# The rope part of the first attention's scores in two passes of the array instead of three

## What is computed

```python
q = (rmsnorm(c_q_raw, q_norm) @ w_uq).reshape(B, S, H, NOPE_DIM + ROPE_DIM)
kv = (rmsnorm(c_kv_raw, kv_norm) @ w_ukv).reshape(B, S, H, NOPE_DIM + V_DIM)
k_nope, v = kv[..., :NOPE_DIM], kv[..., NOPE_DIM:]
q_rope = apply_rope(q[..., NOPE_DIM:], cos[:, :, None, :], sin[:, :, None, :])
k_rope = apply_rope(k_rope_raw, cos, sin)
q_full = jnp.concatenate([q[..., :NOPE_DIM], q_rope], axis=-1)
k_full = jnp.concatenate(
    [k_nope, jnp.broadcast_to(k_rope[:, :, None, :], (B, S, H, ROPE_DIM))], axis=-1)
...
s = jnp.einsum('bqhd,bkhd->bhqk', q_blk, k).astype(jnp.float32) * scale
s = jnp.where(k_idx[None, :] <= q_idx[:, None], s, jnp.finfo(jnp.float32).min)
pr = jax.nn.softmax(s, axis=-1)
```

## Time and profile before

| | |
|---|---|
| median of 3 runs | 1946.9 us (1946.67 to 1947.23) |
| profiled execution, its own time | 1946.78 us |
| its span in the trace | 1945.0 us |
| PE busy | 1925.1 us (99%) |
| DVE busy | 1226.0 us (63%) |
| ACT busy | 898.4 us (46%) |
| POOL busy | 536.3 us (28%) |
| mean clock granted to TensorE | 0.999 of full |

### The profile page before, as it was taken

One profiled execution on the slowest core, in us unless ns is written; L12 is line 12 of the kernel. 1 busy time (PEld: TensorE's weight loads), 2 busy tenths in 40 slices (PEclk: granted clock), 3 DMA queues, 4 the chain that ended last, 5 costly groups with the idle time before them and its releaser, 6 DMA issues.

```text
span 1945.0 us, 23730 instructions
## 1 busy us (share of the span) xinstructions
PE 1925.1 (99%) x9278; PEld 1605.7 (83%) x9278; DVE 1226.0 (63%) x1697; ACT 898.4 (46%) x1309; POOL 536.3 (28%) x396
## 2 busy tenths in 40 slices
PE   8999999999999999999999999999999999999998
PEld 7777878888888888888888888888888888888886
DVE  6657676538236845545455857667666676766757
ACT  7445543424235442525255544434455555444435
POOL 2333552251415435353533000000333341000000
PEclk9999999999999999999999999999999999999999
DMA  5312356575532323231315657364322226746553
GB/s 165 95 44 76 101 122 161 136 150 141 101 108 87 109 66 109 66 108 65 108 65 152 155 154 188 109 184 120 108 86 86 86 66 184 181 122 173 127 176 87
DMA packets 164690, 229.70 MB, mean 118 GB/s; under 512 B 4784, under 2 KB 108976, under 8 KB 164464
## 3 DMA queue, kind: packets, MB, share of 16 engines
q1 hardware_dynamic: 148192, 195.24, 32.7%
q0 software_dynamic: 16096, 32.01, 9.5%
q10 hardware_dynamic: 304, 1.12, 0.2%
HBM read 223.23 MB, written 4.72 MB: 117 GB/s over the span
## 4 chain that ended last, share of the span: by engine, by line
PE 94%; DVE 3%; ACT 2%; issue 0%; DMA 0%; SPq 0%; POOL 0%; ACTq 0%; DVEq 0%
PE ps L1150 30%; PE ps L1151 29%; PE ps L1152 29%; PE ps L1322 1%; PE ps L1352 1%; PE ps L1361 1%; PE ps L1362 1%; ACT scr L2255 1%; PE ps L1339 1%; PE ps L1855 0%; DVE x L3243 0%; DMA raw<-in_w_in 0%; DVE hid_lo L3089 0%; DVE hn_lo L3247 0%; ACT w_hi L2008 0%
## 5 line engine op out<-in xcount | busy, mean ns | idle before, releaser
L1150 PE MATMUL ps<-hn_hi,w_hi 128*128 128x512 f32 (+1 forms) x1556 | 607.6, 391 | 4.0 <-DVE hn_lo L3192 1.7
L1152 PE MATMUL ps<-hn_hi,w_lo 128*128 128x512 f32 (+1 forms) x1556 | 599.5, 385 | 0.0
L1151 PE MATMUL ps<-hn_lo,w_hi 128*128 128x512 f32 (+1 forms) x1556 | 599.4, 385 | 0.0
L1004 POOL TENSOR_TENSOR w_lo<-raw,w_hi 128x512 fp32r<-128x512 f32 x244 | 343.0, 1438 | 517.8 <-ACT w_hi L2000 517.8
L1150 PEld LDWEIGHTS ps<-hn_hi,w_hi 128*128 128x128 f32 x1556 | 292.7, 188 | 66.4 <-issue 4.8
L1152 PEld LDWEIGHTS ps<-hn_hi,w_lo 128*128 128x128 f32 x1556 | 292.5, 188 | 59.3
L1151 PEld LDWEIGHTS ps<-hn_lo,w_hi 128*128 128x128 f32 x1556 | 292.8, 188 | 57.2 <-issue 1.4
L1150 PE MATMUL ps<-w_hi,hid_hi 128*128 128x512 f32 x616 | 240.0, 390 | 0.2
L1151 PE MATMUL ps<-w_lo,hid_hi 128*128 128x512 f32 x616 | 239.7, 389 | 0.0
L1152 PE MATMUL ps<-w_hi,hid_lo 128*128 128x512 f32 x616 | 239.7, 389 | 0.0
L2044 ACT ACTIVATE w_hi<-raw 128x1024 fp32r<-128x1024 f32 x112 | 116.1, 1055 | 205.7 <-PE ps L1152 205.4
(11 more groups left out here) (383 smaller groups left out, 2902.7 us busy)
## 6 DMA issues: line engine op xcount, KB each, us to landing
raw<-in_mlp_w SPq DMA_DIRECT2D x56, 1024.0 KB, 5.5
raw<-in_ret_w_in SPq DMA_DIRECT2D x24, 1024.0 KB, 5.1
aux<-in_mlp_w POOLq DMA_DIRECT2D x16, 1024.0 KB, 9.2
raw<-in_att_w_in SPq DMA_DIRECT2D x12, 1024.0 KB, 5.3
raw<-in_w_gate SPq DMA_DIRECT2D x11, 1024.0 KB, 5.4
raw<-in_w_up SPq DMA_DIRECT2D x11, 1024.0 KB, 5.3
raw<-in_w_down SPq DMA_DIRECT2D x9, 1024.0 KB, 5.2
raw<-in_ret_w_out SPq DMA_DIRECT2D x8, 1024.0 KB, 5.1
```

The source lines that it names most:

```text
L1004: ins = pool.tensor_tensor(w_lo[:, slot, at], raw[:, slot, at], w_hi[:, slot, at].bitcast(F32), ALU.subtract)
L1150: pe.matmul(o, hi, rhs_hi, start=start, stop=False, skip_group_check=True)
L1151: pe.matmul(o, hi, rhs_lo, start=False, stop=False, skip_group_check=True)
L1152: return pe.matmul(o, lo, rhs_hi, start=False, stop=stop, skip_group_check=True)
```

## The change

The rope rows of each query head are laid out anew: 32 rows of the high part and under them the 32 rows of the low part, in the 64 partitions of that head's half (`Q_ROPE`, `q_rope_rows`). Since the rope key's high part lies in all four quarters, one pass of 64 rows now gives high by high and low by high together, and a second pass of 32 rows gives high by low. To write this layout, ACT makes one full high copy per group of four heads into `sq_halves` (`rope_hi`) and four copies of 32 partitions (`rope_hi_rows`), and DVE makes four subtractions of 32 partitions (`rope_low`) where it had one of 128. The order of the steps on both engines changes too, and so do PE's waits ahead of tile 3 of pairs 0 and 2.

```diff
--- before.py
+++ after.py
@@ -535,6 +535,13 @@
         att_squares = [tab[:, 0, :], aux[:, 0, :], aux[:, 1, :], tmp[:, 1, :]]
         Q_NOPE_LO = (hid_hi[:, 2, :], hid_hi[:, 3, :], hid_lo[:, 2, :], hid_lo[:, 3, :])
 
+        Q_ROPE = (hid_hi[:, 9, :], hid_lo[:, 9, :], hid_hi[:, 10, :], hid_lo[:, 10, :])
+
+        def q_rope_rows(h, low):
+
+            at = 64 * (h % 2) + 32 * low
+            return Q_ROPE[h // 2][at:at + 32, :]
+
         def head_values(j):
 
             both = (hid_hi, hid_lo)[j // 2][:, 12 + 2 * (j % 2):14 + 2 * (j % 2), :]
@@ -596,9 +603,8 @@
                 r, q, k = self.rows(b), self.p, 4 + self.p
                 q_hi, q_lo = probs_t[r, q, :], Q_NOPE_LO[q][r, :]
                 nope = [(q_hi, hid_hi[r, k, :]), (q_hi, hid_lo[r, k, :]), (q_lo, hid_hi[r, k, :])]
-                r, q = slice(32 * (h % 4), 32 * (h % 4) + 32), 9 + h // 4
-                rope = [(hid_hi[r, q, :], hid_hi[r, 8, :]), (hid_hi[r, q, :], hid_lo[r, 8, :]),
-                        (hid_lo[r, q, :], hid_hi[r, 8, :])]
+                r = self.rows(b)
+                rope = [(Q_ROPE[self.p][r, :], hid_hi[r, 8, :]), (q_rope_rows(h, 0), hid_lo[64 * b:64 * b + 32, 8, :])]
                 return [nope, rope]
 
             def v_both(self, b, j):
@@ -1333,7 +1339,7 @@
                 for nth in range(2):
                     for t in tiles:
                         parts = [a.qk(b)[1 - nth] for b in range(2)]
-                        for n in range(3):
+                        for n in range(len(parts[0])):
                             for b in range(2):
                                 q, k = parts[b][n]
                                 ins = pe.matmul(a.score_ps(b, t), q[:, t * P:(t + 1) * P], k[:, 0:(t + 1) * P],
@@ -1388,7 +1394,9 @@
                     pe.wait_ge(pair_free[g.pair], g.freed(p % 2))
                     if p == 0:
                         pe.wait_ge(s["krep_done"], 96)
-                        pe.wait_ge(s["qr_lo"], 2)
+                    if p % 2 == 0:
+                        pe.wait_ge(s["qr_hi"], p + 2)
+                        pe.wait_ge(s["qr_lo"], p // 2 + 1)
                     g = UQ.group(2 + p // 2)
                     pe.wait_ge(pair_free[g.pair], g.freed(p % 2))
                     pair_scores(ONES[p], (3,))
@@ -2231,7 +2239,13 @@
             def rope_hi(r):
 
                 act.wait_ge(s["q_rope"], r + 1)
-                act.activation(hid_hi[:, 9 + r, :], tmp[:, r, :], ACT.Copy).then_inc(s["qr_hi"], 1)
+                act.activation(sq_halves[:, r, :], tmp[:, r, :], ACT.Copy).then_inc(s["qr_hi"], 1)
+
+            def rope_hi_rows(r):
+
+                for n in range(4):
+                    ins = act.activation(q_rope_rows(4 * r + n, 0), tmp[32 * n:32 * n + 32, r, :], ACT.Copy)
+                ins.then_inc(s["qr_hi"], 1)
 
             def nope_hi(n):
 
@@ -2242,9 +2256,11 @@
                         .then_inc(s["q_nope_hi"], 1)
 
             rope_hi(0)
+            rope_hi_rows(0)
             nope_hi(0)
             rope_hi(1)
             nope_hi(1)
+            rope_hi_rows(1)
             split(CONVS.chunk(1))
 
             def pair_exps(a, b):
@@ -3048,13 +3064,22 @@
                     dve.tensor_tensor(Q_NOPE_LO[tile], ps[:, g.bank(m), :], probs_t[:, tile, :].bitcast(F32),
                                       ALU.subtract).then_inc(pair_free[g.pair], 1)
 
+            def rope_low(r):
+
+                dve.wait_ge(s["q_rope"], r + 1)
+                dve.wait_ge(s["qr_hi"], 2 * r + 1)
+                for n in range(4):
+                    rows = slice(32 * n, 32 * n + 32)
+                    ins = dve.tensor_tensor(q_rope_rows(4 * r + n, 1), tmp[rows, r, :],
+                                            sq_halves[rows, r, :].bitcast(F32), ALU.subtract)
+                ins.then_inc(s["qr_lo"], 1)
+
+            rope_low(0)
             nope_low(0)
-            for r in range(2):
-                dve.wait_ge(s["q_rope"], r + 1)
-                dve.wait_ge(s["qr_hi"], r + 1)
-                dve.tensor_tensor(hid_lo[:, 9 + r, :], tmp[:, r, :], hid_hi[:, 9 + r, :].bitcast(F32),
-                                  ALU.subtract).then_inc(s["qr_lo"], 1)
             nope_low(1)
+            rope_low(1)
+            dve.wait_ge(s["qr_hi"], 4)
+            dve.wait_ge(s["qr_lo"], 2)
 
 
             def pair_masked(a, tiles, at=MASK_AT):
```

## The result

| | before | changed |
|---|---|---|
| median of 11 runs | 1946.9 us (1946.34 to 1948.14) | 1951.88 us (1950.35 to 1953.25) |
| ratio, 95% interval | | 1.0023 [1.0016, 1.0031] |
| profiled execution, its own time | 1946.78 us | 1950.35 us |
| its span | 1945.0 us | 1948.2 us |
| time less span | 1.8 us | 2.15 us |

The account below looks back on a forecast made before the run. PE, busy 99% of the span, was taken as the bound. Each pair: +0.53 us in tiles 2, 0 and 1, -0.23 in tile 3; four pairs add +1.2 to 1946.8, giving 1948.0 us, range 1944.2 to 1950.8.

Parts of the forecast that it names:

- DVE, before the first masks: Six more DVE subtractions, 3.6 us, mostly fill idle time; masks start some 0.5 us later, PE waits for nothing: price nothing.
- the third: DVE's rope subtractions run beside POOL, masks end at 89.6, PE waits 5.8 us before tiles 2, 0, 1: 1953.8 us; 4%.
- The price of one 32-partition subtraction: On DVE ahead of the first masks: each added subtraction priced at 0.60 us, six making 3.6 us.
- The masks: On DVE: first mask starts near 81.9 us with no idle time ahead, and PE shows no wait for it.
- An ACT copy of 32 partitions: On ACT: in a row every 0.5 us or so, eight new ones about 4 us, the first four from 72.1 to 74.2.
- The switch: On PE: changing a pass's row count costs 0.20 us, about 0.10 ahead to empty the array and 0.11 behind for loads.
- the rope stretch: Tiles 2, 0 and 1 of each pair, first rope to first nope pass: 1.94 us against 1.41, +0.53 us.
- tile 3: Tile 3 of each pair: switches stay three, one 512-column pass falls away, -0.23 us; 1.56 us instead of 1.79.
- Rival 1: Switches between 64 and 32 rows nearly free among rope passes: -0.63 us a pair, -2.5 us in all, 1944.3 us; 12%.
- Rival 2: Switches in close succession cost about 0.35 us instead of 0.20: 3.0 us more over four pairs, 1951.0 us; 8%.
- ACT's and POOL's delays: ACT's split of convolution chunk 1 and POOL's low part move some 2.1 us later, covered by idle time: price nothing.

Follow-up runs that it names:

- The run with DVE's part alone: Kernel before, with the rope subtractions cut into eight of 32 partitions, four ahead of nope and four behind: median 1950.3 us, ratio 1.0015.
- the run without waits: Changed kernel with DVE doing nope of heads 0-3, both rope groups, tile 3's masks, then nope of heads 4-7: median 1948.6 us, ratio 1.0008.
- nope ahead of rope: Changed kernel with DVE doing the two nope subtractions of heads 0 to 3 ahead of the four rope ones: median 1953.5 us, ratio 1.0033.
- the grouped kernel: Changed kernel with the rope passes of tiles 2, 0 and 1 ordered three of 32 rows, then three of 64: median 1948.8 us, ratio 1.0009.

## Why the prediction was wrong

**The step that failed** is "DVE, before the first masks". It priced the delay of the nope subtractions at nothing, with the sentence that the first nope group's banks come free at 78.2, "also in time". I checked that against tile 3, which wants them at 79.35, and not against what PE does ahead of it. The first convolution product starts at 76.53 and writes into these very banks. They came free at about 75.9 before the change, 0.6 us ahead of it, which no list of waits showed. The four rope subtractions in front took 2.8 us; DVE began them 0.25 us earlier than it had begun nope, so nope came 2.55 us later (77.19 against 74.64). Between the end of nope and PE's next start pass 0.15 us in the changed kernel, so the margin was 0.45 us, and 2.55 - 0.45 = 2.1 us is by how much the product starts later (78.63 against 76.53). The run with DVE's part alone shows the wait (2.02 us), and the run without waits shows 0.25 us left at this place when nope stands first.

**The rival that was nearest** was the third: DVE late, PE waits. I had it at 4%, at the wrong place (ahead of tile 2) and only through POOL. Its mechanism is real: nope ahead of rope ran into it, with the last two subtractions at 1.2 us each and a wait of 1.76 us.

**The price of one 32-partition subtraction** in a row was 0.69 us (2.77 for four), not the 0.60 that I took from the pitch of the 128x512 ones. The masks were forecast for 81.9; DVE was free for them at 82.5. In the changed kernel this cost nothing, because PE was late by then. An ACT copy of 32 partitions in a row was mis-sized too: the first four took 2.54 us (71.97 to 74.51), 0.63 each and not "0.5 us or so", and pushed the nope copies from 74.02 to 74.53. In the changed kernel DVE was busy with rope until 77.19, so nobody waited for them. Where nope stands first, it is the 0.25 us at the first convolution product.

**The clock was missing from the sum.** It has no term for it, as if the granted clock were 1.00 throughout, which it is in that stretch of the kernel before. Behind a new pause of PE of 1.8 to 2.1 us, five of eight profiles show it at 1.2 GHz for 3 to 7 us; behind 4.8 us the one profile does, and behind 0.6 us the one profile doesn't. In the changed kernel it costs 1.5 to 1.6 us where it happens, and by the mean clocks on record it happened in 8 of 24 executions. The Trainium skill says in "TensorE: Matmul & The Clock Gate", section "Why this matters for your kernels", that long idle gaps between bursts of matmuls bring the clock back down. The gaps that it names are longer than the ones of 1.8 to 2.1 us here, and behind these the clock fell all the same, to 0.58 in the stretch from 80 to 84 us of the grouped kernel; so here the measurement decides.

**What was right.** The switch as the cost that eats the gain: 1.88 us for the rope stretch (1.94 forecast), 1.55 for tile 3 (1.56). A pair costs 0.47 - 0.24 = +0.23 us by these, so +0.9 in four (+1.2 forecast). The lag behind the kernel before is 2.10 us at the first convolution matmul (78.63 against 76.53) and 3.06 us at the matmul near 189 us (191.75 against 188.69), so 0.96 us came in between, as these passes say. Rival 1 (the switch is nearly free) is refuted by grouping: the same passes in another order are 2.6 us faster. Rival 2 (a switch at 0.35 us) as well: none of them is dearer than 0.20. ACT's and POOL's delays cost nothing in the changed kernel, as said.

**The sum over the change**, then: 1.0 us of switches less passes, 2.25 us by the wait, 0.5 us of clock on average (1.5 to 1.6 us in a third of the executions), 0.1 to 0.8 us that the four profiles have behind 189 us, and 0.3 us outside the span. That makes 4.2 to 4.9 us, against 4.5 and 5.0 by the medians and 4.1 and 4.6 by the means of the same runs. The share of the clock is an estimate, from the mean clock of each execution, which is on record to three digits only. Two terms have no cause shown: the part behind 189 us, which the kernel without waits has too (0.4), and the time less span, which is 2.1 to 2.2 us in each kernel with the stacked rows and 1.8 to 1.9 in those without.

## What to carry to other kernels

When work is put in front of an instruction that frees PSUM banks, look for the next writer of those banks in PE's order, whatever it belongs to; it may be a product that has nothing to do with the change, and a small margin there shows in no list of waits. Merging passes of small row counts can pay only if passes of one row count stay together: the same six rope passes took 1.88 us a pair when they alternated and 1.10 when they were grouped, against 1.41 for the nine before. Even then the median showed no gain here. And a pause of PE of about 2 us can cost more than its length, since the clock may fall behind it: 1.5 to 1.6 us more than the 2.1 in the changed kernel, about 2.9 more than the 1.76 in the one with nope first, and nothing more behind the 1.70 us near 189 us.

## What the hardware showed that I had not expected

- A change of row count between 32, 64 and 128 costs 0.16 to 0.20 us, nearly as much as a whole pass of 512 columns (0.23 us), in both directions, even when the next rows are part of those just used.
- The clock fell to 1.2 GHz behind pauses of only 1.76 to 2.12 us, in some executions of one and the same kernel and not in others (8 of 24 of the changed kernel, 6 of 6 with nope first), at once or up to 1.4 us behind the pause, and stayed there for 3 to 7 us. Behind a pause of 1.70 us at another place it never fell.
- A DVE subtraction of 32x512 with all operands in SBUF takes 0.69 us in a row and 1.2 to 1.44 us beside POOL; one of 128x512 with an operand in PSUM keeps its 0.6 us: two take 1.28 us in the kernel without waits from 82.73 on, where POOL is at work from 81.37 for 5.02 us, and 1.29 elsewhere.
